# Output projection of an encoder layer: six of eight token tiles as pairs with seven block products

## The reference

```python
    m = gates[:, :, 0] * (ya @ wa) + gates[:, :, 1] * (yb @ wb) + gates[:, :, 2] * (yc @ wc)
    x = x + rms_norm(m @ w_out, post_g)

    x = x + jax.nn.sigmoid(x @ w_pg) * (p_i @ w_pe)
    return x
```

## Time and profile before

| | us |
|---|---|
| Median of 3 runs | 1332.19 (1331.86 to 1332.44) |
| Span of the profiled execution | 1330.3 |
| TensorE busy | 1312.1 |
| VectorE busy | 680.8 |
| ScalarE busy | 575.5 |
| GpSimd busy | 352.0 |

### The profile page before, as it was taken

How to read it: one execution, slowest core, us unless ns; L and a number is a source line. 1 busy time by engine, 2 the same in 40 slices (tenths; PEclk the granted TensorE clock), 3 DMA queues, 4 the chain that set the end, 5 groups by cost and what they waited for, 6 DMA issues and landing times.

```text
span 1330.3 us, 17488 instructions
## 1 busy us (share of the span) xinstructions
PE 1312.1 (99%) x6636; PEld 1072.0 (81%) x6636; DVE 680.8 (51%) x1285; ACT 575.5 (43%) x1106; POOL 352.0 (26%) x239
## 2 busy tenths in 40 slices
PE   8999999999999999999999999999999999999998
PEld 6788877888888778788888888888877888888887
DVE  6354655556522677786633435555557337435222
ACT  6355455553222577676422245555554223223210
POOL 4122212222434311130244512221211443213100
PEclk9999999999999999999999999999999999999999
DMA  6111112111111200000111211111001114422111
GB/s 214 63 41 41 46 36 57 52 32 52 49 48 32 67 30 16 17 20 21 52 52 32 81 61 33 51 51 42 32 24 41 48 40 167 140 81 70 58 40 40
DMA packets 25712, 72.18 MB, mean 54 GB/s; under 512 B 2808, under 2 KB 4728, under 8 KB 25504
## 3 DMA queue, kind: packets, MB, share of 16 engines
q1 hardware_dynamic: 25632, 71.09, 16.9%
HBM read 66.86 MB, written 4.23 MB: 53 GB/s over the span
## 4 chain that ended last, share of the span: by engine, by line
PE 90%; DVE 4%; ACT 3%; issue 1%; DMA 1%; POOL 1%; SPq 0%; ACTq 0%; DVEq 0%; POOLq 0%
PE ps L934 18%; PE ps L953 14%; PE ps L1290 13%; PE ps L1548 7%; PE ps L1528 6%; PE ps L1175 5%; PE ps L1342 5%; PE ps L1331 2%; PE ps L973 2%; PE ps L1112 2%; PE ps L1028 2%; PE ps L1260 2%; PE ps L1554 2%; PE ps L1406 2%; PE ps L1143 1%; PE ps L1234 1%
## 5 line engine op out<-in xcount | busy, mean ns | idle before, releaser
L728 POOL TENSOR_TENSOR w_lo<-stage,w_hi 128x1024 fp32r<-128x1024 f32 (+2 forms) x84 | 190.3, 2265 | 577.5 <-ACT w_hi L1598 577.5
L1598 ACT CAST w_hi<-stage 128x1024 fp32r<-128x1024 f32 (+2 forms) x92 | 91.3, 992 | 198.0 <-PE ps L934 125.9
L2148 DVE TENSOR_TENSOR pt_lo<-ps,pt_hi 128x512 fp32r<-128x512 f32 (+2 forms) x160 | 97.1, 607 | 80.6 <-ACT pt_hi L1962 40.3
L953 PE MATMUL ps<-h_hi,w_hi 128*128 128x512 f32 x272 | 110.3, 405 | 0.0
L934 PE MATMUL ps<-h_hi,w_hi 128*128 128x512 f32 x352 | 108.9, 391 | 0.7 <-POOL w_lo L728 0.7
L934 PE MATMUL ps<-h_lo,w_hi 128*128 128x512 f32 x352 | 108.5, 389 | 0.0
L934 PE MATMUL ps<-h_hi,w_lo 128*128 128x512 f32 x352 | 108.4, 389 | 0.0
L1290 PE MATMUL ps<-h_hi,w_hi 128*128 128x512 f32 x256 | 106.8, 417 | 0.0
L953 PE MATMUL ps<-h_hi,w_lo 128*128 128x512 f32 x272 | 106.2, 391 | 0.0
L953 PE MATMUL ps<-h_lo,w_hi 128*128 128x512 f32 x272 | 106.1, 390 | 0.0
L1290 PE MATMUL ps<-h_hi,w_lo 128*128 128x512 f32 x256 | 100.5, 392 | 0.0
(11 more groups left out here) (386 smaller groups left out, 3059.3 us busy)
## 6 DMA issues: line engine op xcount, KB each, us to landing
stage<-in_w_gates SPq DMA_DIRECT2D x24, 512.0 KB, 3.6
stage<-in_w_qkvg_a SPq DMA_DIRECT2D x19, 512.0 KB, 4.4
stage<-in_w_qkvg_c SPq DMA_DIRECT2D x16, 512.0 KB, 3.6
m<-in_x_tok SPq DMA_DIRECT2D x8, 512.0 KB, 6.4
stage<-in_w_branch SPq DMA_DIRECT2D x8, 512.0 KB, 3.7
y_plain<-in_x_tok SPq DMA_DIRECT2D x8, 512.0 KB, 3.7
stage<-in_w_pg SPq DMA_DIRECT2D x16, 256.0 KB, 3.0
out<-y_plain SPq DMA_DIRECT2D x16, 256.0 KB, 2.0
```

The costliest lines, as they stand in the source:

```text
L728: nc.gpsimd.tensor_tensor(dst, stage[:, staged, 0:width], f32(hi), ALU.subtract).then_inc(w_ready, 1)
L953: done = mm(ps[:, half_bank(T), :], w[:, slot, k * P:(k + 1) * P], h[:, k, g * SEQ:(g + 1) * SEQ], start=k == 0 and part == 0, stop=k == K ...
L1598: nc.scalar.copy(dst, stage[:, staged, 0:width]).then_inc(w_hi_done, 1)
L2148: sub = lambda out, whole, hi: nc.vector.tensor_tensor(out, whole, f32(hi), ALU.subtract)
```

## The change

Tiles 0 and 1 are multiplied as before (`out_plain`, 48 matmuls each), with operand units in `w_hi`/`w_lo` in place of q and k. A unit is one half of a tile's channels (the even or the odd chunks, 4 x 128), split in two parts; there are four slots for units, and unit u waits for the end of product u-4. Tiles 2 to 7 go in three pairs. Two tiles by two channel halves are a 2x2 block matrix, the output weights another (even or odd chunks, left or right 512 columns), and the product is made in the Strassen-Winograd form: seven products of 12 matmuls, with four sums of blocks of `m` (GpSimd) and four sums of weight blocks (VectorE, once, 16 operations, `out_weight_sums`; their parts go to free buffers). VectorE and ScalarE add the seven results up (`saved0`, `take`), quarter by quarter. The normalisation works from these quarters in SBUF, two tiles after another. The operands aren't halved any more; the variance is taken with 4 x EPS instead. SyncE loads x back over the finished tile of `m`, and the gate weights only after the weight sums. The split of turned tile 0 comes after the last pair on ScalarE and VectorE. The core of the diff, added lines only (`gate_weights` is a split of one eighth of the gate weights, `out_rstd` the power, `out_var` and `out_norm` the variance and the two operations of the normalisation, `split_unit` waits for a unit's high part and makes the low one):

```diff
+O_PAIRS = 3
+O_UNITS = 4 + 7 * O_PAIRS
+SLOT_OF = [1, 3, 0, 2]
+ROLES = [(0, 1, 4), (4, 0, 1), (1, 4, 0)]
+QUARTERS = [(0, 0), (1, 0), (1, 1), (0, 1)]
+TAKEN_AT = [1, 4, 6, 7]
+def out_unit(u):
+    if u < 4:
+        return u // 2, u % 2, None
+    p, i = divmod(u - 4, 7)
+    tile, side = [(0, 0), (0, 1), (1, 1), (1, 1), (0, 0), (1, 0), (0, 1)][i]
+    return 2 * p + 2 + tile, side, None if i < 3 else 2 * p + (1 if i == 3 else 2)
...
+        def unit_parts(u, chunks=slice(0, UNITS)):
+            slot = SLOT_OF[u % 4]
+            cols = slice(slot % 2 * SEQ, slot % 2 * SEQ + SEQ)
+            return [w[:, slot // 2, cols].rearrange("p (c q) -> p c q", q=P)[:, chunks, :] for w in (w_hi, w_lo)]
+        def unit_raw(u, chunks=slice(0, UNITS)):
+            tile, side, _ = out_unit(u)
+            return m[:, tile, side::2, :][:, chunks, :]
+        def role_bank(p, i):
+            a, b, c = ROLES[p]
+            return [a, b, 2, 3, c, a, b][i]
...
+            sp.wait_ge(block_done, LEAD + N_MERGE[2] + 14)
+            sp.dma_start(post_gain, post_g.broadcast_to([P, D])).then_inc(g_in, 16)
+            def load_x_again(t):
+                sp.wait_ge(unit_ready, LEAD + max(u for u in range(O_UNITS) if out_unit(u)[0] == t) + 1)
+                if t >= 2:
+                    sp.wait_ge(x2_ready, LEAD + x2_count(t - 2))
+                sp.dma_start(x_row(t), x_tok[t]).then_inc(xr_in[t % 2], 16)
+            for t in range(2):
+                load_x_again(t)
+            sp.wait_ge(w_sums, LEAD + 1)
             for c in range(2):
+                load_w(N_PG[0] + c, c, w_pg[c])
+            for p in range(O_PAIRS):
+                for c in range(2):
+                    load_w(N_PG[0] + 2 * p + 2 + c, c, w_pg[2 * p + 2 + c])
+                for t in (2 * p + 3, 2 * p + 2):
+                    load_x_again(t)
+            sp.wait_ge(unit_done, LEAD + O_UNITS - 4)
...
+                load_w(N_PE + c, c, w_pe[1 - c])
...
+            def first_units(p):
+                a11, a12, a21, a22 = four_blocks(p)
+                for i in range(3):
+                    split_unit(4 + 7 * p + i, wait=True)
+                nc.gpsimd.tensor_tensor(a22, a21, a22, ALU.add).then_inc(unit_sums, 1)
+                pool.wait_ge(unit_sums, LEAD + 2 * p + 1)
+            def other_units(p):
+                u = 4 + 7 * p
+                a11, a12, a21, a22 = four_blocks(p)
+                steps.done(pool, nc.gpsimd.tensor_tensor(a21, a11, a21, ALU.subtract))
+                steps.done(pool, nc.gpsimd.tensor_tensor(a11, a22, a11, ALU.subtract))
+                nc.gpsimd.tensor_tensor(a12, a12, a11, ALU.subtract).then_inc(unit_sums, 1)
+                pool.wait_ge(unit_sums, LEAD + 2 * p + 2)
+                for i in range(4, 6):
+                    split_unit(u + i)
...
+            pool.wait_ge(first_hi_done, LEAD + 1)
+            for u in range(2):
+                unit_lo(u, slice(0, 3), first_ready)
+            for u in range(2):
+                pool.wait_ge(unit_hi_done, LEAD + u + 1)
+                unit_lo(u, slice(3, 4))
+            for u in range(2, 4):
+                split_unit(u)
+            gate_weights(0)
+            out_rstd(0)
+            gate_weights(1)
+            first_units(0)
+            for p in range(O_PAIRS):
+                split_unit(4 + 7 * p + 3)
+                out_rstd(2 * p + 1)
+                other_units(p)
+                gate_weights(2 * p + 2)
+                split_unit(4 + 7 * p + 6)
+                gate_weights(2 * p + 3)
+                if p < O_PAIRS - 1:
+                    first_units(p + 1)
+                out_rstd(2 * p + 2)
+            out_rstd(2 * O_PAIRS + 1)
+            for k in range(2):
+                split_w(N_PE + k, k, dst=w_lo[:, 1 - k, :], hi=w_hi[:, 1 - k, :])
...
+                for i, which in enumerate(["11", "21", 4, 1, 2, 3, "22"]):
+                    u, bank = 4 + 7 * p + i, role_bank(p, i)
+                    if p == 0 and i == 0:
+                        pe.wait_ge(merged, LEAD + 3 * KC)
+                    elif i >= 5:
+                        pe.wait_ge(*[(first_saved, LEAD + p + 1), (taken, LEAD + 7 * p + 1)][i - 5])
+                    elif p == 0 and i == 4:
+                        pe.wait_ge(x2_ready, LEAD + 1)
+                    elif p:
+                        pe.wait_ge(taken, LEAD + 7 * (p - 1) + [2, 3, 4, 6, 7][i])
+                    if p == 0 and which in (1, 2, 3, 4):
+                        pe.wait_ge(w_sums_ready, LEAD + {4: 4, 2: 8, 3: 12, 1: 16}[which])
+                    pe.wait_ge(unit_ready, LEAD + u + 1)
+                    hi, lo = unit_parts(u)
+                    for c in range(UNITS):
+                        w_hi_part, w_lo_part = out_state(which, c)
+                        for part, (a, w) in enumerate([(hi, w_hi_part), (hi, w_lo_part), (lo, w_hi_part)]):
+                            done = mm(ps[:, bank, :], a[:, c, :], w, start=c == 0 and part == 0,
+                                      stop=c == UNITS - 1 and part == 2)
+                    done.then_inc(unit_done, 1)
+                    if p == O_PAIRS - 1 and i == 5:
+                        turn_x2(0)
...
+            for t in range(2):
+                out_plain(t)
+            for p in range(O_PAIRS):
+                seven_products(p)
...
+            def unit_hi(u, chunks=slice(0, UNITS)):
+                sums = out_unit(u)[2]
+                if u >= 4:
+                    act.wait_ge(unit_done, LEAD + u - 3)
+                if sums:
+                    act.wait_ge(unit_sums, LEAD + sums)
+                nc.scalar.copy(unit_parts(u, chunks)[0], unit_raw(u, chunks)).then_inc(unit_hi_done, 1)
+            def sums_hi(k):
+                for c in range(UNITS):
+                    src, hi, _ = sum_home[k, c]
+                    nc.scalar.copy(hi, src).then_inc(w_sums_hi_done, 1)
...
+            for u in range(2):
+                unit_hi(u, slice(3, 4))
+            act.wait_ge(block_done, LEAD + N_MERGE[2] + 16)
+            for u in range(2, 4):
+                unit_hi(u)
+            act.wait_ge(w_sums, LEAD + 1)
+            sums_hi(4)
+            for u in range(4, 6):
+                unit_hi(u)
+            gate_weights(0)
+            sums_hi(2)
+            square_plain(0)
+            gate_weights(1)
+            sums_hi(3)
+            for u in range(6, 8):
+                unit_hi(u)
+            for c in range(UNITS):
+                nc.scalar.copy(half(h_hi[:, 2 * c, :], 1), first_sum[c]).then_inc(w_sums_hi_done, 1)
+            square_plain(1)
+            for p in range(O_PAIRS):
+                u = 4 + 7 * p
+                act.wait_ge(unit_done, LEAD + u + 1)
+                act.wait_ge(w_sums_ready, LEAD + 4 * UNITS)
+                act.wait_ge(taken, LEAD + 7 * p)
+                nc.scalar.copy(saved0, ps[:, role_bank(p, 0), :]).then_inc(first_saved, 1)
+                unit_hi(u + 4)
+                unit_hi(u + 5)
+                square_quarter(p, 0)
+                gate_weights(2 * p + 2)
+                unit_hi(u + 6)
+                gate_weights(2 * p + 3)
+                if p < O_PAIRS - 1:
+                    for i in range(7, 10):
+                        unit_hi(u + i)
+                for i in range(1, 3):
+                    square_quarter(p, i)
+                if p < O_PAIRS - 1:
+                    unit_hi(u + 10)
+                square_quarter(p, 3)
...
+            turned_hi(0)
+            for k in range(2):
+                act.wait_ge(unit_done, LEAD + O_UNITS - 1 + k)
+                split_w(N_PE + k, k, N_PE // 2 + 1, dst=w_hi[:, 1 - k, :])
...
+            def out_weight_sums(c):
+                if c == UNITS - 1:
+                    for k in range(2):
+                        dve.wait_ge(w_in_slot[k], 16 * (N_OUT // 2 + 1))
+                even, odd = out_raw[2 * c], out_raw[2 * c + 1]
+                t2, t3, t4 = [sum_home[k, c][0] for k in (2, 3, 4)]
+                steps.done(dve, nc.vector.tensor_tensor(t3, half(odd, 1), half(even, 1), ALU.subtract))
+                steps.done(dve, nc.vector.tensor_tensor(t2, t3, half(even, 0), ALU.add))
+                nc.vector.tensor_tensor(first_sum[c], half(even, 1), half(even, 0), ALU.subtract)
+                return nc.vector.tensor_tensor(t4, half(odd, 0), t2, ALU.subtract)
+            def sums_lo(j, k):
+                for c in range(UNITS):
+                    src, hi, lo = sum_home[k, c]
+                    dve.wait_ge(w_sums_hi_done, LEAD + UNITS * j + c + 1)
+                    sub(lo, src, hi).then_inc(w_sums_ready, 1)
...
+            for c in range(UNITS):
+                done = out_weight_sums(c)
+                if c < UNITS - 1:
+                    steps.done(dve, done)
+            done.then_inc(w_sums, 1)
+            sums_lo(0, 4)
+            sums_lo(1, 2)
+            out_var(0, 0)
+            sums_lo(2, 3)
+            out_norm(0, 0, banks(4))
+            for c in range(UNITS):
```

(62 more changed lines are left out.)

248 lines of the change are left out of this document (115 added, 133 removed).

## The result

The changed kernel takes **1370.18 us** (median of 4 runs, 1369.5 to 1371.54), the kernel before 1332.24 (4 runs of the same comparison, 1331.86 to 1332.44): a ratio of 1.0287, interval 1.0273 to 1.0302. It is slower by 38 us; the forecast was 1371. The profiled execution is the fastest of the four: it has a span of 1367.5 us and a time of 1369.5; before's has a span of 1330.3.

A forecast was written before the change was run, and what follows sets the result against it. The prediction took TensorE to bound the kernel, busy 99% of the span. Saved matmuls (-8.2 us) and added waits summed to +35.3, with the clock +38.8 on a 1332.19 us median: forecast 1371 us, range 1342 to 1388.

The forecast's parts named there:

- walk: Following the new queues in program order with the earlier trace's durations, port to whoever asked first; sum +35.3 us before clock.
- (f): Clock after long waits: cold restart about 1.7 us, paid in full at the embedding, partly elsewhere; +3.5 us.
- (a): Tiles 0 and 1: GpSimd's splits interleave with VectorE's last merge operations, delaying the seventh block and tile 1; +2.2 us.
- (b): First product: weight sums, then gate weights, hold operand 4 on GpSimd's queue; tile 1's cover is used up; +10.4 us.
- (c): Inside pair 0: fourth product waits for low parts of sums, +2.6 us; fifth for operand 8, +5.2 us.
- (d): Pairs 1 and 2: GpSimd's power and three sums wait for the previous pair's normalisations; +4.9 us each, 9.8 us.
- (e): Step to the embedding: turned tile 0 is split only after both of pair 2's normalisations; +13.3 us.
- What goes: Matmuls in the three pairs: 84 in place of 96 each, 36 fewer at 0.2267 us; -8.2 us.
- rival C: Operands are in time, operand 4 ready by 1143.4, so only the matmuls count: 1324 us, faster; chance 0.05.
- Rival A: VectorE and GpSimd run beside each other after all, without port exclusion: about +10, 1342 us; chance 0.09.
- Rival B: Clock stays low, the pairs' 84 products at half rate: up to +36 us more, 1385 to 1405 us; chance 0.07.

The follow-up runs named there:

- filled kernel: Changed kernel with extra matmuls while TensorE waits: 40 before the first seven-block product, 14 before each fifth product, 50 before the embedding; 1367.08 us.
- PSUM operands: Changed kernel with norms and additions of tiles 2 to 5 reading a PSUM bank in place of the SBUF copy of their product; 1362.18 us.
- sums-first kernel: Changed kernel with GpSimd computing the inverse norm of each pair's odd tile behind its three operand sums instead of ahead of them; 1366.23 us.
- the kernel with the tail in another order: Changed kernel with VectorE and ScalarE splitting turned tile 0 of the embedding ahead of the last two normalisations; 1363.23 us.
- both kernels with all the reorderings: Changed kernel with operand splits earlier in the head, GpSimd's sums before the power, and turned tile 0 split earlier: 1357.60 us; also with norms reading PSUM: 1350.53 us.

## Why the prediction was right, point by point

The walk of the prediction ran at full clock and priced the clock apart, in (f). The kernel with filled holes is the one that shows the walk's own quantities: all waits at a clock of 1.00, the filler counted as waiting. In us, over the pitch, less the 0.5 that was there before; (f) is what all slow matmuls add up to:

| step | walked | filled kernel | changed kernel |
|---|---|---|---|
| (a) tile 0 and 1 | 2.2 | 1.0 | 1.0 |
| (b) first product | 10.4 | 10.0 | 10.0 |
| (c) fourth product | 2.6 | 2.05 | 0 |
| (c) fifth, pair 0 | 5.2 | 4.8 | 3.9 |
| (d) fifth, pairs 1 and 2 | 4.9 each | 4.4 each | 3.9 each |
| (e) embedding | 13.3 | 13.45 | 13.5 |
| sum of the waits | 43.5 | 40.1 | 36.1 |
| (f) clock | 3.5 | 0 | 8.5 |

- **What goes**, -8.2: 36 matmuls at 0.2267, as said.
- **(a)** The merge and the splits interleaved as walked; the 0.7 us at tile 1 didn't appear, and the first hole was half a microsecond shorter. This term was 1.2 us too large.
- **(b)** The sums ended at 1144.19 (walked 1144.5); the first product started at 1155.76 (walked 1156.5). Doubling the sums gave 11.1 us more hole, so "the cover is used up by the sums" is shown. What the walk didn't see: the order on GpSimd's queue, on which rival C leaned, is only the last of two late things. In another order 9.6 of the 9.9 us came back at the fourth product.
- **(c), (d)** The chains are those named, each term 0.4 to 0.55 us too long against the filled kernel. The fourth product's is further off: of its 2.05 us there, 1.0 is the port turn that fell otherwise than in the changed kernel. Where the pairs' terms are too long can be read in the chain of the changed kernel: from the end of pair 0's last product (1182.6) the first normalisation runs to +5.9 (walked +6.1), but the three sums take 5.7 us (1189.43 to 1195.1), where 6.3 was walked. Two of them take some 0.85 us more than the first, beside VectorE's normalisation. That the port, and not the number of steps, makes most of these holes is shown by the PSUM operands: 3.7 to 1.0 and 1.5.
- **(e)** The order is the cause: 11 us of the hole went with the order alone, and 2.1 came back one step on.
- **(f)** That the clock falls, and that a later wait covers part of a restart, came out. The size didn't. The prediction takes 1.7 us for the embedding and half of 1.7 for three others, which is 4.25 and not 3.5; with that the forecast would have been 1372. Measured are 5.0: 1.4 at the embedding, and 1.04, 1.05 and 1.52 of the 1.6 us in each pair, which is over two thirds and not half. Nothing is left of the first product's 2.2, as said. In the trace 8.5 us of slow matmuls stand, since 3.0 of them lie where TensorE would otherwise have waited; that is why the changed kernel's waits (36.1) are shorter than the walk's. Whoever adds all 8.5 to the walked waits counts these twice.

So the mechanism is right in each part, and that the sum came within 1 us is partly luck. Without its own port turn the filled kernel's waits are 39.1 us, so the walk is 4.4 too long. Against that the clock is 1.5 too small, 0.66 us of later start stands in no term, and neither does the 0.1 us that each restart costs at full clock, 0.7 in all. What is left is 1.6 us between the spans (38.8 forecast, 37.2 measured) and 0.8 between forecast and median.

Rival A (no contention) fell with the rows of 2.2 to 3.4 us beside GpSimd. Rival B (a clock that stays low) fell too: behind each hole of the changed kernel matmuls are back at 0.227 within 5 us. Rival C asked for an operand by 1143.4; it came 12 us later.

What stays open: why the sums-first kernel spreads over 5 us from run to run. Port turns that fall one way or the other, as seen above, are a cause that would do; I have one trace of it only, so this is not shown. Also open is what the form costs with the sums of output weights out of the head; no run shows that.

## What to carry to other kernels

Fewer matmuls are worth only what the engines that prepare their operands can keep up with: work out, per product saved, the time on the port that VectorE and GpSimd share, counting VectorE's operations with two SBUF inputs and not those with a PSUM input, before counting the matmuls. Walk each queue in its order from the first operand, and when a reordering removes a wait, ask for the next late operand at once: here it was 10 us late too. Price each hole with the clock behind it, and take off only what a later wait really covers.

## What the runs showed of the chip that I had not expected

- TensorE's granted clock can fall after the hole is over. Behind two of the changed kernel's holes of 3.9 us it was still 1.00 when work began again: it fell at 1174.0, with TensorE at work from 1172.74, and at 1197.9, with work from 1197.39. Behind the third it had fallen just before (1221.8, work from 1222.03), and behind the holes of 10 and 13 us it was at 0.50 from the first matmul.
- The length of a hole didn't tell the cost of the restart. The slow matmuls added 2.1 us behind a hole of 20.97 us (the doubled sums), 2.9 behind one of 3.70 (the kernel with the tail in another order) and 1.5 to 1.7 behind most. Holes of 0.87, 1.00 and 1.51 us were followed by no slow matmul; of eight holes of 2.09 to 2.60 us five were (two in the kernel with the tail in another order) and three were not (the 2.38 above, and the 2.31 before the embedding in both kernels with all the reorderings).
- Two instructions that want the shared port within 0.01 us of each other can be served either way (1.23 and 2.37 us, or 2.35 and 1.28), in kernels whose VectorE and GpSimd queues up to there are the same. The start in the trace doesn't tell who is served: with PSUM operands GpSimd's sum starts at 1159.73, VectorE's addition at 1159.74, and the addition went first. This alone moved a product by 0.9 us.
